# Other matrix work moved inside the attention steps of a fused two-block kernel: between the two turns of probabilities, or right behind the values

## The reference, cut to what matters

```
p = u @ w_in
q, k, v = heads of p ; q, k normalised and rotated ; k_all, v_all = context keys and values before those of x
attn = softmax(q k_all^T / 8) v_all * silu(p[za])         # 8 query heads, 2 key heads, 512 queries, 768 keys
u2   = a * sigmoid(g)                                     # 512 channels
y    = depthwise_conv(u2, 31 taps) + conv_b
y    = silu(layer_norm(y, ln_w, ln_b))                    # mean and variance over the 512 channels
conv = (y @ w_pw + b_pw) * silu(p[zc])
h    = x + gate * (concat(attn, conv) @ w_out)
```

## Time and profile before

| | |
|---|---|
| runs | 1092.59, 1093.66, 1094.22 us; median 1093.66 |
| span of the profiled execution | 1094.2 us (no other time is given for it) |
| TensorE busy | 1056.6 us, 97% |
| VectorE busy | 649.6 us, 59% |
| ScalarE busy | 455.0 us, 42% |
| attention steps 0 to 18 | about 176 to 284 us of the span |
| mean granted TensorE clock | 0.997 |

### The profile page before, as it was taken

One profiled execution on the slowest core, in us unless ns is written; L12 is line 12 of the kernel. 1 busy time (PEld: TensorE's weight loads), 2 busy tenths in 40 slices (PEclk: granted clock), 3 DMA queues, 4 the chain that ended last, 5 costly groups with the idle time before them and its releaser, 6 DMA issues.

```text
span 1094.2 us, 22599 instructions
## 1 busy us (share of the span) xinstructions
PE 1056.6 (97%) x9830; PEld 828.2 (76%) x9830; DVE 649.6 (59%) x1019; ACT 455.0 (42%) x738; POOL 5.6 (1%) x10
## 2 busy tenths in 40 slices
PE   8999998988999999999999999999999999999998
PEld 6777776776787777777777767787888888888887
DVE  4569898966467665868676757654443223444222
ACT  5344554677325543443535235344442112443111
POOL 0000000000000000000000000000000000000000
PEclk9999999999999999999999999999999999999999
DMA  9812124000522210110110121242233332333330
GB/s 359 357 61 96 58 97 173 1 1 2 192 100 75 76 40 22 41 40 23 40 33 31 41 78 42 70 142 80 94 97 104 98 99 84 96 96 96 97 106 29
DMA packets 26161, 94.99 MB, mean 87 GB/s; under 512 B 2896, under 2 KB 3152, under 8 KB 25552
## 3 DMA queue, kind: packets, MB, share of 16 engines
q1 hardware_dynamic: 26064, 93.54, 25.3%
HBM read 89.34 MB, written 4.19 MB: 85 GB/s over the span
## 4 chain that ended last, share of the span: by engine, by line
PE 77%; DVE 13%; ACT 4%; issue 3%; DMA 2%; SPq 1%; POOL 0%; ACTq 0%; DVEq 0%
PE psum L841 20%; PE psum L843 19%; PE psum L842 19%; DVE work L2007 3%; PE psum L851 3%; DMA ring<-weights 2%; PE psum L1270 2%; PE psum L1257 2%; PE psum L982 1%; PE psum L1026 1%; PE psum L1329 1%; PE psum L1306 1%; DVE small_temps L2194 1%; PE psum L1062 1%; PE psum L1283 1%
## 5 line engine op out<-in xcount | busy, mean ns | idle before, releaser
L2063 DVE TENSOR_TENSOR weights_low<-ring,weights_high 128x1024 fp32r<-128x1024 f32 x70 | 85.8, 1226 | 75.4 <-ACT weights_high L1617 75.4
L1617 ACT ACTIVATE weights_high<-ring 128x1024 fp32r<-128x1024 f32 x70 | 73.7, 1052 | 127.6 <-PE psum L843 127.6
L841 PE MATMUL psum<-normed_high,weights_high 128*128 128x512 f32 x256 | 101.5, 397 | 0.1
L843 PE MATMUL psum<-normed_high,weights_low 128*128 128x512 f32 x256 | 101.1, 395 | 0.0
L842 PE MATMUL psum<-normed_low,weights_high 128*128 128x512 f32 x256 | 101.1, 395 | 0.0
L842 PE MATMUL psum<-hidden_low,weights_high 128*128 128x512 f32 x256 | 99.6, 389 | 0.0
L843 PE MATMUL psum<-hidden_high,weights_low 128*128 128x512 f32 x256 | 99.6, 389 | 0.0
L841 PE MATMUL psum<-hidden_high,weights_high 128*128 128x512 f32 x256 | 99.6, 389 | 0.0
L2007 DVE SCALAR_TENSOR_TENSOR work<-work,small_sb 128x512 f32<-128x512 f32 x116 | 80.1, 747 | 0.1
L1587 ACT ACTIVATE work<-psum 128x384 f32<-128x384 f32 (+1 forms) x116 | 56.9, 540 | 53.3 <-PE psum L982 23.0
L841 PE MATMUL psum<-pair_normed_high,pair_weights_high 128*128 128x512 f32 x176 | 75.5, 429 | 0.8 <-DVE normed_low L2067 0.8
(11 more groups left out here) (319 smaller groups left out, 2130.8 us busy)
## 6 DMA issues: line engine op xcount, KB each, us to landing
ring<-weights SPq DMA_DIRECT2D x135, 512.0 KB, 3.6
work<-weights SPq DMA_DIRECT2D x10, 512.0 KB, 13.2
residual<-xT SPq DMA_DIRECT2D x4, 512.0 KB, 6.3
mixed<-weights SPq DMA_DIRECT2D x4, 512.0 KB, 7.7
residual_saved<-residual SPq DMA_DIRECT2D x8, 256.0 KB, 4.4
residual<-residual_saved SPq DMA_DIRECT2D x1, 2048.0 KB, 9.1
outT<-residual SPq DMA_DIRECT2D x8, 256.0 KB, 3.2
tables_sb<-tables SPq DMA_DIRECT2D x1, 1280.0 KB, 13.3
```

The source lines that it names most:

```text
L841: pe.matmul(out, wh, high(k), start=first and n == 0, stop=False)
L843: ins = pe.matmul(out, wl, high(k), start=False, stop=last and n == len(order) - 1)
L1617: act.activation(wsplit(q)[0], room_of(b), ACT.Copy).then_inc(w_high, 1)
L2063: vec.tensor_tensor(low, room_of(b), high.bitcast(F32), ALU.subtract).then_inc(w_low, 1)
```

## The change

Two predicates say where a step's other work stands. In steps whose work is a `cmean` or a `pw` (5 to 8 and 15 to 18) it goes between the turn of head 0 and the turn of head 1, and the values come last. In the steps of `spread0` to `spread2` (9, 12, 14) it goes right behind the values, ahead of the turn of head 1. Steps 0 to 4, 10, 11 and 13 keep their order. The list of PSUM names is put in the same order. The programs of the other engines are not edited.

```diff
+def amid_turns(u):
+    return BESIDE_ATTENTION.get(u, ("",))[0][:2] in ("cm", "pw")
+
+def behind_values(u):
+    return u in SPREAD_AT
...
                 t, v = u - TURN_LAG, u - VALUE_LAG
                 if 0 <= t < STEPS:
                     turn_probs(t, 0)
+                if amid_turns(u):
+                    beside_attention(u)
+                    if 0 <= t < STEPS:
+                        turn_probs(t, 1)
                 if u == STEPS + VALUE_LAG - 1:
                     spread_inverse(NQ - 1)
                 if v >= 0:
...
                     value_pair(v, o)
-                if 0 <= t < STEPS:
-                    turn_probs(t, 1)
-                beside_attention(u)
+                if behind_values(u):
+                    beside_attention(u)
+                if not amid_turns(u):
+                    if 0 <= t < STEPS:
+                        turn_probs(t, 1)
+                    if not behind_values(u):
+                        beside_attention(u)
```

The same in the list of PSUM names, where the last name of the attention steps is now `spread3` (bank 2) instead of `pw3` (bank 7):

```diff
-        if u == STEPS + VALUE_LAG - 1:
-            o.append((f"spread{NQ - 1}", 1, 2))
-        if u in BESIDE_ATTENTION and BESIDE_ATTENTION[u][1] == 0:
-            o.append((BESIDE_ATTENTION[u][0], 1, 7))
+        turned(0)
+        if amid_turns(u):
+            beside()
+            turned(1)
+        if u == STEPS + VALUE_LAG - 1:
+            o.append((f"spread{NQ - 1}", 1, 2))
+        if v >= 0 and v % QT == 0:
+            o.append((f"o{v // QT}", 1, 6))
+        if behind_values(u):
+            beside()
+        if not amid_turns(u):
+            turned(1)
+            if not behind_values(u):
+                beside()
```

More of the change, by code:

```diff
@@ L270, in psum_order, with turned, beside @@
         t, v = u - TURN_LAG, u - VALUE_LAG
-        for h in range(2):
+        def turned(h):
             if 0 <= t < STEPS:
[L273 to L276, removed]
+                o.extend((f"pt{t}_{h}_{x}", 1, 4 + x) for x in range(2))
+        def beside():
+            if u in BESIDE_ATTENTION and BESIDE_ATTENTION[u][1] == 0:
+                o.append((BESIDE_ATTENTION[u][0], 1, 7))
+        turned(0)
+        if amid_turns(u):
+            beside()
+            turned(1)
         if u == STEPS + VALUE_LAG - 1:
             o.append((f"spread{NQ - 1}", 1, 2))
-        if u in BESIDE_ATTENTION and BESIDE_ATTENTION[u][1] == 0:
-            o.append((BESIDE_ATTENTION[u][0], 1, 7))
+        if v >= 0 and v % QT == 0:
[6 more added lines that the diff above has]
+                beside()
     add(*(f"out{m}" for m in range(5)), "mem_sum", *(f"out{m}" for m in range(5, DK)))
```

## The result

The changed kernel takes 1100.66 us (median of 4 runs, 1098.86 to 1101.68) against 1093.80 us (4 runs, 1092.59 to 1094.22) for the kernel before: ratio 1.0062, 95% interval 1.0049 to 1.0074, which is 6.8 us slower (5.4 to 8.1). The profiled execution has a span of 1099.9 us and a time of its own of 1101.68.

What follows compares the result with a forecast made beforehand. TensorE, 97% busy, was taken as the bound, so only waits on its path counted: 0.34 + 1.92 + 2.82 + 1.16 = 6.24 us on 1093.66 gave 1099.9 us, range 1096.5 to 1102.5.

Steps and rivals of the forecast that it cites:

- Part 1: Steps 5 to 7: `cmean` between the turns makes no wait, and VectorE's taps set the path; no change.
- Part 2: Step 8: `cmean` waits for the last convolution sum and delays step 9's scores; +0.34 us.
- Part 3: Steps 9, 12, 14: moved `spread0` to `spread2` find bank and inputs ready, the filled hole returns at step 15's scores; nothing.
- The rival on the clock: New holes in TensorE's work bring its clock down, 0.9 or 1.8 us lost; 1101.7 us; chance 0.08.
- Part 4: Step 15: `pw0` waits for bank 7 until VectorE's reader of `spread2`, behind the row maxima, frees it; +1.92 us.
- Part 5: Steps 16 and 17: `pw1` and `pw2` each wait for the earlier `pw`'s reader to free bank 7; +1.41 us each.
- Part 6: Start of the output product: tiles wait for `gated_low`, as `pw3` no longer covers VectorE's work; +1.16 us, between 0 and 2.
- What else moves: Later load of the memory tokens and unpinned banks from `out0` to `kks_1` shifted by three: both covered, nothing.

Runs made afterwards that it cites:

- e9_spread2_back: The changed kernel with only `spread2` (step 14) back at its old place, at the step's end; 1099.40 us, 1.0049 of the kernel before.
- e1_cmean: The changed kernel cut down to the moves of the `cmean`s, `spread`s and `pw`s as in the kernel before; 1093.22 us, 1.0004 of the kernel before.
- e8_rotate: The kernel before with only the unpinned banks of `out0` to `kks_1` shifted by three; 1092.58 us, 1.0000 of the kernel before.
- e2_spread: The changed kernel cut down to the moves of `spread0` to `spread2`; 1093.60 us, 1.0006 of the kernel before.
- e11_spread2: The kernel before with only `spread2` moved, right behind step 14's values; 1093.62 us, 1.0003 of the kernel before.
- e10_kept2: The changed kernel with steps 8, 18 and `spread2` in old order, `pw1`/`pw2` in banks 0/1, `spread2`'s reader ahead of step 15's row maxima; 1091.52 us, ratio 0.9984.
- e4_banks: The changed kernel with `pw1` and `pw2` in banks 0 and 1 instead of 7; 1098.14 us, 1.0044 of the kernel before.

## Why the prediction was right, and where it was off

The forecast was 1099.9 us, in a range of 1096.5 to 1102.5, by a mechanism of four waits; measured was 1100.66. `e9_spread2_back`, which has all moves but the one that brings the clock down, is the cleanest measure of the mechanism: 6.30 us from A to B against a sum of 6.24. Timed, its three runs without any fall have a mean of 1098.00 us, the ten such runs of the kernel before beside them 1091.74: 6.26. Its three runs with one fall have 1100.60 against 1092.94 (14 runs), 7.66, so the timed runs bear the sum out within about a microsecond; the tenths rest on the trace.

**Part 1, `cmean` in steps 5 to 7: nothing.** Right: from step 5's scores to A takes 18.87 us in `e1_cmean` and 18.87 in `e8_rotate`, though TensorE reaches step 8's scores 0.26 us sooner in `e1_cmean` (15.99 against 16.25 us behind step 5's); VectorE's taps set the pace, as the forecast says.

**Part 2, step 8: +0.34.** Right, 0.30: the sum starts at 217.95, `cmean` 0.75 us later, the scores of step 9 3.17 us behind that.

**Part 3, the `spread`s: nothing.** This step failed. I followed what `spread2` needs, found it ready, and took the hole that it fills to come out again one place later. It does (0.78 and 1.30 for 1.66 and 0.28), but I did not ask what the two holes on either side of a lone turn do to the clock. That cost 0.88 us in the changed kernel (against `e9_spread2_back`) and 1.53 in `e2_spread`; step 9 gave back 0.15. The rival on the clock had it, with new holes in TensorE's work as its cause and 0.9 to 1.8 us as its price, at 0.08, and I argued it down with a stretch of the kernel before that looked just as idle and kept its clock. That one profile was weak evidence, as `e11_spread2` shows from the other side. The median, 1100.66, lies between the forecast and this rival's 1101.7.

The Trainium skill (TensorE: Matmul & The Clock Gate, Part 1: The HAM clock gate) states that the number of slow matmuls at a kernel's start varies between runs of the same kernel. The runs here show the like further on: the counts of falls above differ from run to run of each kernel.

**Part 4, `pw0`: +1.92.** Right, but to be seen only where the clock stays up. From s15 to `pw0` takes 3.86 us in `e9_spread2_back` and 1.97 in `e10_kept2`, where nothing is waited for: 1.89. In the changed kernel it is 4.72, of which 0.86 is the slow clock: TensorE came late to a bank that had freed itself meanwhile, so the bracket shows only 1.04.

**Part 5, `pw1` and `pw2`: +1.41 each.** The chain is as forecast: 4.32 us from the second turn to the next `pw` (269.65 - 265.33) against 4.39. The distance between `pw`s grew by 1.50, since a `pw` that had to wait occupies TensorE for 3.70 instead of 3.60 us by its row, and 3.54 instead of 3.43 from its start to the next turn (269.65 to 273.19 in the changed kernel, 267.72 to 271.15 in `e4_banks`). That term was missing, 0.1 us for each of three `pw`s.

**Part 6, start of the output product: +1.16.** The waits stand where the sum put them: S is 286.89, the first tile S + 2.57 (forecast 2.49), the second S + 3.89 (3.90), and the sixth, whose `gated_low(5)` stands behind `pw3`'s reader, 293.84, S + 6.95 (7.00). With step 18 in its old order and no waits, the stretch from `pw2` to M is 25.20 - 23.56 = 1.64 us shorter (`e9_spread2_back` and `e10_kept2`), 0.1 of it the longer `pw2`, so the new order of step 18 costs some 0.4 us more than forecast; which of its rows holds that is open. That is given back where the new order has shorter seams, 0.30 us from s15 to M. I had counted neither.

**What else moves.** Nothing, as forecast: `e8_rotate` has the banks alone and is within 0.1%, and the stretch from M to B, where a late load of the memory tokens would show, takes 99.74 us in the changed kernel and 99.79 in the kernel before.

That the sum came out at 6.24 for a measured 6.30 is in part luck, as small errors cancel: 0.3 us too little for the matmuls behind a wait and 0.4 for the output product, against 0.45 us of seams that no rule of mine had.

## What to carry to other kernels

A filler pays where the engine waits now (what other orders gave here was half a microsecond in all, from shorter seams), and where both its inputs and its place for the result are ready at the new time: work back from there through the queue of the engine that frees the bank (here ScalarE's copies, its weights, VectorE's low part, the reader). Where several waits appear, take them away one at a time, by a bank or by the order of the reader; a wait can hide a second loss, which shows only when the first is gone. And ask of each hole that is cut in two what it does to TensorE's clock, over many runs and not over one profile.

## What the runs showed of the hardware

A fall of the clock is a matter of chance for a given order of work. It takes the mean granted clock to 0.83 over the 10 us in which it lies (190 to 200 us in the kernel before), occurs at four places of this kernel, and most of the scatter between runs is its doing: the 75 runs of the kernel before spread by 1.36 us (standard deviation), and by 0.75 us once 1.5 us per fall is taken off. Comparing only runs with as many falls is a sharper test than comparing medians.

A `pw` behind a wait takes 0.1 us longer (3.70 against 3.60 us by its row). The wait is not the only thing that does it: `pw3`, which stands right behind values and not behind a turn, has 3.70 in every kernel here, with no wait ahead of it. The order of matmuls of different kinds is worth 0.05 to 0.1 us at a seam (1.36 against 1.46, 3.43 against 3.53, 0.75 against 0.81 us start to start, as above).
